# Attention on TensorE: value products of two jobs in every second slot, short scores in pairs

## The reference

```python
# A: 4 heads, q and k in two halves of 64, values of 128 columns
p = softmax(q_m @ k_m.T + bias, masked by chunk)         # m = 0, 1
out = (p_0 - lam * p_1) @ v                              # then an rms norm of each row
# B: 8 heads of 64, a band of the last chunks, with a sink in the softmax
out = softmax_with_sink(q @ k_band.T + bias) @ v_band
# C: 8 heads of 64, one key and value head, keys chosen by an index score
out = softmax(q @ k.T + bias, chosen keys only) @ v
y = sum_n sigmoid(h @ w_gate_n + b_n) * (branch_n @ w_branch_n); x = x + y @ w_out
```

## Time and profile before

| what | value |
|---|---|
| time, median of 3 runs | 1469.86 us (1468.39 to 1470.03) |
| the profiled execution | 1467.45 us, of which span 1465.7 us |
| TensorE busy | 1400.4 us, 96% of the span, mean granted clock 0.993 |
| VectorE, GpSimd, ScalarE busy | 51%, 53%, 34% |
| attention stage of layer 0, of layer 1 | 173 to 442 us, 975 to 1244 us |

### The profile page before, as it was taken

One profiled execution on the slowest core, in us unless ns is written; L12 is line 12 of the kernel. 1 busy time (PEld: TensorE's weight loads), 2 busy tenths in 40 slices (PEclk: granted clock), 3 DMA queues, 4 the chain that ended last, 5 costly groups with the idle time before them and its releaser, 6 DMA issues.

```text
span 1465.7 us, 19408 instructions
## 1 busy us (share of the span) xinstructions
PE 1400.4 (96%) x6786; PEld 1015.7 (69%) x6786; DVE 746.7 (51%) x1937; ACT 501.1 (34%) x1190; POOL 773.2 (53%) x651
## 2 busy tenths in 40 slices
PE   6999999999999999999589999999999999899996
PEld 5788777777777865565376887777777778565553
DVE  4487775546675155222146687655457543452221
ACT  4322333333432133343243332333343413243341
POOL 5556554443445525667555565444434464266663
PEclk9999999999999999999899999999999999999999
DMA  7435322223212848999632242222232147689993
GB/s 199 118 118 152 87 65 83 70 64 99 85 58 72 288 165 286 326 347 338 167 115 78 58 117 84 77 62 79 79 97 73 58 146 258 206 273 336 327 337 101
DMA packets 148563, 225.30 MB, mean 154 GB/s; under 512 B 18480, under 2 KB 95722, under 8 KB 148458
## 3 DMA queue, kind: packets, MB, share of 16 engines
q1 hardware_dynamic: 136264, 198.58, 42.4%
q0 software_dynamic: 9648, 16.81, 4.8%
q10 hardware_dynamic: 2546, 8.57, 1.5%
HBM read 216.51 MB, written 31.25 MB: 169 GB/s over the span
## 4 chain that ended last, share of the span: by engine, by line
PE 43%; DVE 3%; DMA 1%; POOL 1%; issue 1%; ACT 1%; SPq 0%; POOLq 0%; DVEq 0%
PE bank L802 9%; PE bank L804 9%; PE bank L803 9%; PE bank L1052 8%; PE bank L967 2%; PE bank L978 1%; PE bank L999 1%; PE bank L1038 1%; PE bank L989 1%; PE bank L922 1%; PE bank L1194 0%; DMA X<-residual_dram 0%; DMA residual_dram<-mixed,slot_token 0%; PE bank L935 0%; POOL w_lo L755 0%
## 5 line engine op out<-in xcount | busy, mean ns | idle before, releaser
L689 POOL TENSOR_SCALAR w_hi<-raw 128x1024 fp32r<-128x1024 f32 (+2 forms) x144 | 150.7, 1047 | 455.6 <-PE bank L804 450.9
L693 POOL TENSOR_TENSOR w_lo<-raw,w_hi 128x512 fp32r<-128x512 f32 (+2 forms) x288 | 360.3, 1272 | 12.0
L803 PE MATMUL bank<-w_hi,hT_lo 128*128 128x512 f32 (+2 forms) x704 | 261.6, 372 | 0.0
L1052 PE MATMUL bank<-work,ptmp 128*128 128x512 f32 x512 | 225.3, 593 | 2.7 <-ACT ptmp L1390 2.7
L802 PE MATMUL bank<-w_lo,hT_hi 128*128 128x512 f32 (+2 forms) x576 | 216.3, 376 | 3.1 <-POOL w_lo L693 1.4
L804 PE MATMUL bank<-w_hi,hT_hi 128*128 128x512 f32 (+2 forms) x576 | 211.6, 367 | 0.0
L755 POOL TENSOR_TENSOR w_lo<-work,w_hi 128x512 fp32r<-128x512 f32 x128 | 158.2, 1264 | 51.0 <-ACT w_hi L1400 50.9
L1052 PEld LDWEIGHTS bank<-work,ptmp 128*128 128x128 f32 x512 | 94.7, 190 | 110.7 <-issue 107.1
L802 PE MATMUL bank<-hT_lo,w_hi 128*128 128x512 f32 x384 | 159.3, 415 | 0.0
L804 PE MATMUL bank<-hT_hi,w_hi 128*128 128x512 f32 x384 | 150.8, 393 | 0.0
L803 PE MATMUL bank<-hT_hi,w_lo 128*128 128x512 f32 x384 | 150.0, 391 | 0.0
(11 more groups left out here) (293 smaller groups left out, 2351.9 us busy)
## 6 DMA issues: line engine op xcount, KB each, us to landing
work<-in_w_ff_gate SPq DMA_DIRECT2D x66, 512.0 KB
work<-in_w_ff_up SPq DMA_DIRECT2D x66, 512.0 KB
work<-in_w_ff_down SPq DMA_DIRECT2D x33, 1024.0 KB, 6.1
raw<-in_w_gate SPq DMA_DIRECT2D x48, 512.0 KB, 3.9
raw<-in_w_in SPq DMA_DIRECT2D x40, 512.0 KB, 3.8
raw<-in_w_branch SPq DMA_DIRECT2D x24, 512.0 KB, 3.6
raw<-in_w_out SPq DMA_DIRECT2D x16, 512.0 KB, 3.7
normed_dram<-mixed ACTq DMA_DIRECT2D x8, 512.0 KB, 2.6
```

The source lines that it names most:

```text
L689: nc.gpsimd.tensor_scalar(w_hi[:, two, :, 0:w], raw[:, slot, :, 0:w], 1.0, 0.0, ALU.mult, ALU.add).then_inc(split_hi, 1)
L693: last = nc.gpsimd.tensor_tensor(w_lo[:, two, kk, 0:w], raw[:, slot, kk, 0:w], w_hi[:, two, kk, 0:w].bitcast(F32), ALU.subtract)
L803: nc.tensor.matmul(out_ap, s_lo, m_hi, start=False, stop=False)
L1052: last = nc.tensor.matmul(G[e % 2][:, :], et[:, e % 2, kt * P:(kt + 1) * P], work[:, n % RING, kk, :], start=(kt == 0), stop=(kt == KT - 1))
```

## The change

TensorE no longer issues the values of one job in each slot. In even slots s it issues those of jobs s-4 and s-3 together, in odd slots none. For A jobs the two stand ahead of the scores, for B and C behind them. Where both jobs of an even-odd pair have at most 256 keys (A and C with `i` = 0, 1, and all of B), the scores of both are issued in the even slot, the second into columns 256 to 511 of the two `S` banks, with one `s_done` for both; the odd slot then has none. `pv_done` is raised once for two jobs. ScalarE in even slots takes the exponentials before the copy, since the copy now waits for values issued in the same slot. VectorE does both jobs' `rows_out` in the even slot. Amounts of work don't change.

```diff
+def scored_together(g):
+    return JOBS[g | 1].nk <= 2 * P
+SCORED = list(itertools.accumulate(0 if scored_together(g) and g % 2 == 0 else 1 for g in range(N_JOBS)))
+SCORED = [n + (scored_together(g) and g % 2 == 0) for g, n in enumerate(SCORED)]
+def valued(g):
+    return g // 2 + 1
...
             def scores(job):
-                if g:
+                second = scored_together(g) and g % 2 == 1
+                cols = slice(2 * P * second, 2 * P * second + job.nk)
+                if g and not second:
                     pe.wait_ge(soft_done, g)
...
-                last.then_inc(s_done, 1)
+                if second or not scored_together(g):
+                    last.then_inc(s_done, 1)
...
             def times_values(job):
-                    if job.g:
+                    if job.g and job.g % 2 == 0:
                         pe.wait_ge(o_free, job.g)
...
-                last.then_inc(pv_done, 1)
+                if job.g % 2:
+                    last.then_inc(pv_done, 1)
...
...attention() of TensorE
-                    if job_at(s):
+                    ended = [job_at(s - 4), job_at(s - 3)] if s % 2 == 0 and s >= 4 else []
+                    rows_first = bool(ended) and ended[0].name == "A"
+                    for job in ended if rows_first else []:
+                        times_values(job)
+                    if job_at(s) and not (scored_together(s) and s % 2):
                         scores(job_at(s))
-                    if job_at(s - 3):
-                        times_values(job_at(s - 3))
+                        if scored_together(s):
+                            scores(job_at(s + 1))
+                    for job in [] if rows_first else ended:
+                        times_values(job)
...
...copy_turned and attention() of ScalarE
-                    act.wait_ge(pv_done, job.g - 1)
+                    act.wait_ge(pv_done, valued(job.g - 2))
...
+                    if s % 2 == 0 and job_at(s - 1):
+                        exps(job_at(s - 1))
                     if turning:
                         copy_turned(turning, 0)
-                    if job_at(s - 1):
+                    if s % 2 and job_at(s - 1):
                         exps(job_at(s - 1))
...
...soft, rows_out and attention() of VectorE
-                v.wait_ge(s_done, g + 1)
+                v.wait_ge(s_done, SCORED[g])
+                first = 2 * P * (scored_together(g) and g % 2)
...
-                v.wait_ge(pv_done, g + 1)
+                v.wait_ge(pv_done, valued(g))
...
-                        rows_out(ended)
+                        if ended.g % 2:
+                            rows_out(job_at(s - 4))
+                            rows_out(ended)
```

More of the change, by code:

```diff
@@ L1 @@
+import itertools
 import math
@@ L966, in scores @@
                     r = slice(HD * m, HD * (m + 1))
-                    last = nc.tensor.matmul(S[m][:, 0:job.nk], q[r, job.u, job.i * P:(job.i + 1) * P], k[r, keys],
+                    last = nc.tensor.matmul(S[m][:, cols], q[r, job.u, job.i * P:(job.i + 1) * P], k[r, keys],
                                             start=True, stop=True)
-                last.then_inc(s_done, 1)
+                if second or not scored_together(g):
+                    last.then_inc(s_done, 1)
             def turn_probs(job, m):
@@ L1360, in attention @@
                     if ended and ended.pair is not None and ended.i == TT - 1:
-                        act.wait_ge(pv_done, ended.g + 1)
+                        act.wait_ge(pv_done, valued(ended.g))
                         if ended.pair in SPLIT_SLOT:
@@ L1375, in attention @@
                             if n == 2:
-                                act.wait_ge(pv_done, A_JOBS)
-                                act.wait_ge(s_done, A_JOBS + TT * B_HEADS // 2)
+                                act.wait_ge(pv_done, valued(A_JOBS - 1))
+                                act.wait_ge(s_done, SCORED[A_JOBS + TT * B_HEADS // 2 - 1])
                             row = ROW_BGATE + n * KT + c * 4 + t
@@ L1684, in soft @@
                     added = [p[:, m, 0:nk] for m in range(2)]
-                v.wait_ge(s_done, g + 1)
+                v.wait_ge(s_done, SCORED[g])
+                first = 2 * P * (scored_together(g) and g % 2)
                 for m in range(2):
-                    last = nc.vector.tensor_tensor_reduce(p[:, m, 0:nk], added[m], S[m][:, 0:nk], 1.0, least[m], ALU.add, ALU.min,
+                    last = nc.vector.tensor_tensor_reduce(p[:, m, 0:nk], added[m], S[m][:, first:first + nk], 1.0, least[m], ALU.add, ALU.min,
                                                           job_neg[:, g % 4, m:m + 1])
```

## The result

The changed kernel takes 1456.48 us (median of 4 runs, 1455.64 to 1459.62) where the kernel before, on the same chips, takes 1469.12: ratio 0.992, 95% interval 0.9901 to 0.9938, 12.6 us less. The profiled execution took 1456.25 us, its span 1454.5 against 1465.7, 11.2 us less.

What follows compares the result with a forecast made beforehand. TensorE, busy 266 of 269 us in layer 0's attention, was taken as the bound; 18.2 - 2.0 - 2.8 + 0.8 = 14.2 us saved gave 1455.7 us from the median 1469.86, range 1449 to 1465.

Steps and rivals of the forecast that it cites:

- TensorE's list is the time: Attention stage: TensorE busy 266 of 269 us, so each slot lasts as long as TensorE's own list.
- 18.2 us of switching: TensorE in attention: fewer changes of array division save 9.1 us a layer, 18.2 us in all.
- the rows: Profile timeline rows of the kernel before, giving slot overheads of 0.41 to 0.56 us and the 18.2 us saving.
- The count of mode changes at one price: TensorE's switching counted otherwise: 48 fewer changes a layer at 0.21 each, 20.2 us; not adopted.
- Joins are free: Second job of a kind adds only streaming; rival: 40 joins a layer cost 0.11 each, 8.8 us, 1464.5, chance 0.07.
- Odd slots: Odd slots with merged scores shrink from 5.3 to 3.9 us; two waits a layer for VectorE's normalising, 2.0 us in all.
- Slot 7: VectorE, already late in this A slot, ends 1.8 later; wait before slot 8 grows 1.4, 2.8 us for both layers.
- Slot 43: Wait of 0.8 for VectorE shrinks by 0.4 as slots 42 and 43 gain TensorE work: 0.8 us back, both layers.
- ScalarE's copy costs nothing: Even slots: the copy waits for that slot's values, but some 3.4 us of dense work covers it; no cost.
- The price that I gave for lost cover: ScalarE's copy without dense cover: up to 0.6 us in each of 24 even slots, 29 us in both layers.

Runs made afterwards that it cites:

- runs 9 and 10: GpSimd's subtraction left out for gate and branch products (stale low parts), in the whole change (9) and the kernel before (10): 1447.03 and 1464.03 us, one execution each.
- Run 8: Kernel before, with values of B and C jobs moved behind the slot's first dense group, one change of division more: 1481.05 us, ratio 1.0085.
- run 9: Whole change, with GpSimd's subtraction for gate and branch products left out (stale low parts): 1447.03 us, one execution.
- run 7: Whole change, with ScalarE's copy ahead of the exponentials in even slots too: 1470.93 us, ratio 1.0015 to the kernel before.
- run 2: Kernel before, with only the short scores paired and values still one job a slot: 1460.27 us, ratio 0.9933.
- run 1: Whole change, with only the values paired and scores one job a slot: 1470.05 us, ratio 1.0003 to the kernel before.
- run 4: Whole change, with VectorE's last key-ranking round and closing comparison moved from slot 6 to slot 18: 1454.84 us, ratio 0.99 to the kernel before.

## Why the prediction was right

1455.7 us was forecast with 1449 to 1465, and 1456.48 measured; 14.2 us of gain against 12.6. Step by step:

- **TensorE's list is the time.** Right. The stages shrank by 4.6 and 6.6 us, and the span by 11.2.
- **18.2 us of switching.** Right in kind and size. With waits made equal (runs 9 and 10) it is 9.0 us a layer where the rows gave 9.1. Run 8 shows the price from the other side. That a short product pays for its division and not for being short shows in slot 8 of layer 1: six passes of A's values, 128x128 like the transposes ahead of them, take 935.00 - 934.23 = 0.77, six times 0.11 and the 0.1 of going to scores. The count of mode changes at one price, which gave 20.2, is 2 us too high; the rows were the better guide.
- **Joins are free.** Right: 0.86 for 128 and 256 keys in one row of scores, and three tiles of values in 0.80; with 40 joins at 0.11 a layer, runs 9 and 10 would differ by 4.7 and not by 9.0.
- **Odd slots.** Right in mechanism: the slots are 3.9 us, and run 9 shows that what is waited there is VectorE behind GpSimd's subtraction. I had two waits of 0.53 a layer, which is 2.1 in all and not 2.0. There are three in layer 0, before slots 18, 24 and 32, of 0.27, 0.50 and 0.37, and the same in layer 1 with 0.26 in the middle: 1.1 and 0.9. Slots 17 and 31 were foreseen, slot 23 was not. That the sum is 2.0 all the same is in part luck: three smaller waits in place of two larger ones.
- **Slot 7.** Right: the delay before slot 8 grew from 1.15 to 2.51, by 1.4 a layer as summed. From slot 6's first transpose VectorE's chain takes 13.56 us (202.15 to 215.71) instead of 11.71 (203.80 to 215.51), 1.85 for the 1.8 forecast, and TensorE's two slots are 0.5 longer for the 0.4. VectorE got there by another way: the four row squares had one long one (1.35) instead of two (1.36 and 1.34), and the normalising (L1728) was caught now, 1.68 instead of 0.80.
- **Slot 43.** The one term of the sum that failed: the 0.4 us a layer expected back didn't come. The delay before slot 44 is 0.94 before and after. The term let TensorE's slot 42 grow by the values of job 38 and took VectorE's list for fixed. But that list holds branch products, which read banks that the dense work fills, and the dense work stands behind the values:

```profile
402.36 0.69 DVE L1782 SCALAR_TENSOR_TENSOR bank<-mixed,bank 128x512 f32<-128x512 f32 x1
...
403.76 0.69 DVE L1782 SCALAR_TENSOR_TENSOR bank<-mixed,bank 128x512 f32<-128x512 f32 x1
...
405.15 0.69 DVE L1782 SCALAR_TENSOR_TENSOR bank<-mixed,bank 128x512 f32<-128x512 f32 x1
...
409.23 1.79 DVE L1732 TENSOR_SCALAR probs<-probs,job_inv 128x384 f32<-128x384 f32 x2
```

They start 1.40 us apart, the time of six dense MATMUL, where VectorE's own pace was 1.33 before. From slot 42's first transpose, TensorE's two slots take 11.61 us (398.52 to 410.13) instead of 11.33, and VectorE's chain to the end of L1732 12.50 instead of 12.22: both grew by 0.3, so the wait stayed. That VectorE's part was handed on by TensorE is read from these distances; no run tested it. What makes the chain late enough to be waited for is GpSimd again (1.79 for the two L1732): in runs 9 and 10 the delay is gone.

- **ScalarE's copy costs nothing.** Right with the exponentials ahead of it; run 7 shows what it would be otherwise. The price that I gave for lost cover, 29 us, was of the copies themselves, which is not how it would have come.
- **The clock.** Not in the sum: 1.6 us in layer 0. I gave the time of an idle stretch as its length, and behind the 2.5 us before slot 8 there was more, in one of the two layers.

18.2 less 2.0, 2.8 and 1.6 is 11.8, near the 11.2 of the spans. So 2.4 us of the forecast gain did not come, 0.8 from slot 43 and 1.6 from the clock; the medians hide part of it, with 12.6. The 1.4 us between 12.6 and 11.2 are within what single executions differ by (1467.09 to 1470.03 for the kernel before).

## What to carry to other kernels

When an engine is busy all the time, read its list from start to start: products that divide the TensorE array otherwise than their neighbours cost about 0.2 us at each change here, for one key tile or several, so gather those of a kind. Then look for what each slot hid: a pipeline of unequal slots needs every follower's work fitted to the short ones, and a queue's order (the exponentials ahead of a copy that now waits) was worth 14.5 us here, more than the 12.6 that the whole change brought. A wait of the bounding engine can cost more than its length: some 1.6 us on top of 2.5 in most places where the clock fell behind it, and 2.9 in one (run 7).

## What the runs showed of the hardware

- Going between 128x128, 64x128 and 128x64 tiles of the array costs TensorE time beyond the streaming: 0.41 us for a slot with scores, 0.56 with scores and 64-column values, 0.34 for 64-column values alone (run 2), and 0.21 for one change more (run 8). Further products of the same division pay only their streaming. The Trainium skill, "TensorEngine Tiling (Array Packing)", section Key Properties, says that a change of tiling mode drains TensorE, without a figure. The prices above agree with it; what happens inside TensorE at such a change no run here shows.
- Many of VectorE's instructions with SBUF operands alone are held up by GpSimd's subtractions of 1.27 us each: 0.48 for a pair of 128x128 normalisings becomes 1.80 and 1.86 (slot 17, L1732), while its instructions on PSUM stay as they are (0.69 for L1715 on 512 columns). Not all of that kind are: run 4's MAX8 and MATCH_REPLACE8 at 275.51 and 276.31, on SBUF, take 0.68 as ever while a subtraction runs. With the subtractions gone all but the waits behind the blocks of rows vanish in both kernels.
- After idle stretches of TensorE of 2.4 to 2.5 us the granted clock went from 2.4 to 1.2 GHz in some places and not in others: behind slot 8 in layer 0 but not in layer 1 of the changed kernel, in both layers of run 1, in neither of run 7, and there behind slot 44 in both. Behind the shorter waits of the stages, 1.4 us at most (run 4, slot 20), it never fell. What decides between the cases these runs don't show.
